# A hybrid encoder block with hierarchical experts: the routing taken tile by tile, with the engine's eight largest values and their places

## The reference

```python
gl = (xt @ w_group + b_group).astype(jnp.float32)
gp = jax.nn.softmax(gl, axis=-1)
g_onehot = jax.nn.one_hot(jnp.argmax(gl, axis=-1), N_GROUPS, dtype=jnp.float32)
g_w = jnp.sum(gp * g_onehot, axis=-1)
el = (xt @ w_expert + b_expert).astype(jnp.float32).reshape(-1, N_GROUPS, EXPERTS_PER_GROUP)
el_sel = jnp.einsum('nge,ng->ne', el, g_onehot)
ep = jax.nn.softmax(el_sel, axis=-1)
top_w, top_i = lax.top_k(ep, TOP_K)
top_w = top_w / jnp.sum(top_w, axis=-1, keepdims=True)
...
for gi in range(N_GROUPS):
    h = jax.nn.silu(jnp.einsum('nd,edf->nef', xt, w_gate[gi])) * jnp.einsum('nd,edf->nef', xt, w_up[gi])
    y = y + jnp.einsum('nef,efd->nd', h * combine[:, gi, :, None], w_down[gi])
```

## Time and profile before

| | us |
|---|---|
| median of 3 runs | 555.96 |
| lowest, highest | 554.34, 557.6 |
| the profiled execution | 554.07 |
| its span, first to last instruction | 552.0 |
| TensorE busy in it | 448.0 |
| VectorE busy | 108.8 |
| ScalarE busy | 80.7 |
| DMA, moved and mean | 217.68 MB, 394 GB/s |

### The profile page before, as it was taken

The page is one execution under the profiler, slowest core; times in us unless marked ns, Lnnn a source line. Parts: engine busy times, 40 slices in busy tenths (PEclk is TensorE's granted clock), DMA queues, the critical chain, the costliest instruction groups (busy, mean ns, idle before and its releaser), DMA issues.

```text
span 552.0 us, 6408 instructions
## 1 busy us (share of the span) xinstructions
PE 448.0 (81%) x2532; PEld 193.2 (35%) x2532; DVE 108.8 (20%) x348; ACT 80.7 (15%) x217; POOL 28.5 (5%) x61
## 2 busy tenths in 40 slices
PE   9999999999999978559999984952965485665794
PEld 3455554664353332133343521420213121311232
DVE  1028863261140310110210400300021000400012
ACT  1127663221110100000101001000000001000113
POOL 0242412100000000000000000000000000000000
PEclk9999999999999998789999988876877876986998
DMA  8989995969999999999999999999999999999993
GB/s 311 349 326 425 389 343 186 370 249 354 423 421 421 430 425 427 427 430 427 427 426 430 427 425 431 425 430 425 430 429 425 431 425 430 424 431 426 421 397 123
DMA packets 27374, 217.68 MB, mean 394 GB/s; under 512 B 5288, under 2 KB 8104, under 8 KB 13776
## 3 DMA queue, kind: packets, MB, share of 16 engines
q1 hardware_dynamic: 22976, 214.84, 93.8%
q10 hardware_dynamic: 4368, 2.42, 1.5%
HBM read 216.18 MB, written 1.06 MB: 394 GB/s over the span
## 4 chain that ended last, share of the span: by engine, by line
PE 48%; DMA 47%; another core or an unknown queue 2%; SPq 1%; issue 1%; DVE 1%; ACT 0%; DVEq 0%; POOL 0%
DMA ring<-in_w_up_dram 26%; DMA ring<-in_w_gate_dram 21%; PE bank L1478 17%; PE bank L1213 8%; PE bank L1301 5%; PE bank L1503 3%; PE bank L1439 2%; PE bank L1255 2%; PE bank L1279 1%; PE bank L1267 1%; PE bank L1533 1%; PE bank L1551 1%; SPq L340 1%; PE bank L1205 1%
## 5 line engine op out<-in xcount | busy, mean ns | idle before, releaser
L1478 PE MATMUL bank<-ring,head 128*32 128x512 f32 (+1 forms) x992 | 155.3, 677 | 68.8 <-DMA ring<-in_w_gate_dram 38.2
L1478 PEld LDWEIGHTS bank<-ring,head 128*32 128x32 f32 (+1 forms) x992 | 44.6, 128 | 170.0 <-issue 169.9
L1503 PE MATMUL bank<-ring,region_q 128*32 128x512 f32 (+1 forms) x480 | 75.5, 668 | 24.0 <-DMA ring<-in_w_down_dram 23.1
L1081 DVE COPY region_q<-bank 128x256 f32<-128x256 f32 x10 | 4.2, 424 | 300.5 <-PE bank L1457 300.5
L1503 PEld LDWEIGHTS bank<-ring,region_q 128*32 128x32 f32 (+1 forms) x480 | 22.1, 128 | 70.0 <-issue 69.4
L722 ACT ACTIVATE head<-bank 128x512 f32<-128x512 f32 x18 | 9.9, 595 | 238.3 <-PE bank L1533 231.7
L1213 PE MATMUL bank<-ring,head 128*128 128x512 f32 x96 | 43.6, 602 | 0.5 <-DMA ring<-in_w_in_dram 0.5
L1439 PEld LDWEIGHTS bank<-region_q,h 128*128 128x128 f32 x304 | 35.7, 192 | 9.1 <-issue 9.1
L1439 PE MATMUL bank<-region_q,h 128*128 128x128 f32 x304 | 38.5, 279 | 0.0
L1533 PE MATMUL bank<-head,region_q 128*128 128x512 f32 x72 | 33.3, 605 | 1.2 <-ACT head L722 1.2
L1301 PE MATMUL bank<-ring 128*128 128x512 f32 x64 | 29.7, 600 | 0.0
(11 more groups left out here) (198 smaller groups left out, 299.9 us busy)
## 6 DMA issues: line engine op xcount, KB each, us to landing
ring<-in_w_gate_dram SPq DMA_DIRECT2D x28, 2048.0 KB, 39.1
ring<-in_w_up_dram SPq DMA_DIRECT2D x28, 2048.0 KB, 38.9
ring<-in_w_down_dram SPq DMA_DIRECT2D x24, 2048.0 KB, 38.9
ring<-in_w_down_dram SPq DMA_DIRECT2D x12, 1024.0 KB, 13.8
ring<-in_w_up_dram SPq DMA_DIRECT2D x8, 1024.0 KB, 11.9
ring<-in_w_gate_dram SPq DMA_DIRECT2D x6, 1024.0 KB, 10.2
ring<-in_w_o_dram SPq DMA_DIRECT2D x2, 2048.0 KB, 11.9
ring<-in_w_in_dram SPq DMA_DIRECT2D x7, 512.0 KB, 8.0
```

What stands on the lines that cost most here:

```text
L1478: last = pe.matmul(ps[bank][rows, :], xgT[:, c, rows], slots[fill_slot(f + a)][:, c * F:(c + 1) * F], start=(c == 0), stop=(c == KC - 1))
L1503: last = pe.matmul(ps[bank + half][rows, :], hT[:, c, rows], down_cols(slots[fill_slot(f + a)], half, c), start=(c == 0), stop=(c == FC - 1))
```

## The change

VectorE takes tile 0 as soon as its logits are there and then tile 1. The groups' logits lie in a row of eight (`gl8`, padded with -1e30 by a `memset`), the eight largest come from `dve.max`, their places from `dve.max_index`. The places of the group make a mask over the 32 experts, the masked logits go through the same two operations, and the first two places give two one-hot rows (`hots`). `rank_tile(0)` and tile 0's two picks (`first_pick`) stand between tile 1's steps. The two exponentials are asked for together. On TensorE four of the five calls of `multiply_constants` go, tile 0's ranks, counts and the first six chunks of its gather stand ahead of tile 1's. The gathered chunks go to four banks by pairs (`FIRST_BANKS`), with a release for each pair. The order of the experts comes directly behind the picks, the weights and `weigh_picks` behind it. The fourth copy of turned rows goes to ScalarE.

```diff
+            act.wait_ge(h_turned, 4)
+            act.activation(hTr[:, 4:8, P:2 * P], ps[7][:].rearrange("p (c t) -> p c t", c=4), ACT.Copy).then_inc(hTr_act, 1)
+            act.wait_ge(exps_asked, 1)
+            act.activation(g_exp, g_off, ACT.Exp)
+            act.activation(e2, e2, ACT.Exp).then_inc(exps_ready, 1)
...
             def gathered_out(i):
-                act.wait_ge(gathered, 2 * i + (2 if i else 1))
+                if i:
+                    act.wait_ge(gathered, 2 * i + 3)
                 for c in range(4):
-                    last = act.activation(xgT[:, c, :], ps[GD0][:, c * P:(c + 1) * P], ACT.Copy, scale=g2_rows[:, c:c + 1])
+                    if i == 0 and c % 2 == 0:
+                        act.wait_ge(gathered, c // 2 + 1)
+                    last = act.activation(xgT[:, c, :], ps[GD0 if i else FIRST_BANKS[c // 2]][:, c * P:(c + 1) * P], ACT.Copy, scale=g2_rows[:, c:c + 1])
...
-            dve.wait_ge(h_turned, 4)
-            dve.tensor_copy(hTr[:, 4:8, P:2 * P], ps[7][:].rearrange("p (c t) -> p c t", c=4)).then_inc(hTr_dve, 1)
...
+            def best_group(t):
+                return mark(dve.max(g_max8[:, t, :], gl8[:, t, :]))
+
+            def group_place(t):
+                return mark(dve.max_index(g_at[:, t, :], g_max8[:, t, :], gl8[:, t, :]))
...
+            def group_only(t):
+                return mark(dve.scalar_tensor_tensor(here[:, t, :], off_group[:, t, :], NEG, el[:, t, :], ALU.mult, ALU.add))
...
+            k_g = group_logits(1)
+            expert_logits(1)
             after(k_g)
+            k_g = best_group(1)
+            k_rank = rank_tile(0)
             after(k_g)
+            k_g = group_place(1)
+            after(k_rank)
+            first_pick(0, 0)
             after(k_g)
+            k_off = other_groups(1)
+            first_pick(0, 1).then_inc(pick_first, 1)
+            after(k_off)
+            after(group_only(1))
+            after(best_experts(1))
+            after(expert_places(1))
+            two_hots(1).then_inc(hots_ready, 1)
+            dve.wait_ge(hots_ready, 1)
+            choose(1)
...
+            after(rank_tile(1))
+            first_pick(1, 0)
+            first_pick(1, 1).then_inc(pick_ready, 1)
...
             pe.wait_ge(chosen_ready, 1)
+            pe.matmul(ps[RANK0][:, 0:EXPERTS], upper, chosen[:, 0, :], start=True, stop=True).then_inc(ranked, 1)
+            pe.matmul(ps[RANK1][:, 0:EXPERTS], ones, chosen[:, 0, :], start=True, stop=False)
+            pe.matmul(ps[COUNTS][:, 0:EXPERTS], ones, chosen[:, 0, :], start=True, stop=False)
+            pe.matmul(ps[COUNT_COL][0:EXPERTS, 0:1], chosen[:, 0, :], ones[:, 0:1], start=True, stop=False)
+            multiply_constants(1, Y2)
+            pe.wait_ge(pick_first, 1)
+            first_gather(0, range(0, 4))
+            pe.wait_ge(hots_ready, 1)
...
             pe.wait_ge(pick_ready, 1)
+            first_gather(1, range(0, 2)).then_inc(gathered, 1)
+            first_gather(1, range(2, 4)).then_inc(gathered, 1)
+            pe.wait_ge(places_ready, 1)
+            pe.matmul(ps[ORDER][0:1, 128:128 + EXPERTS], expert_col, place_hot[0:EXPERTS], start=True, stop=True).then_inc(ordered, 1)
...
             first_gate(range(0, 4))
+            first_gather(1, range(4, 6)).then_inc(gathered, 1)
+            first_gather(0, range(6, KC))
+            first_gather(1, range(6, KC)).then_inc(gathered, 1)
             pe.wait_ge(xg_mid, 1)
```

More of the change, by code:

```diff
@@ new lines, in _ @@
+            k_w = mark(dve.tensor_scalar(w1, e2, 1.0, None, ALU.add))
+            after(k_key)
+            k_key = mark(dve.tensor_reduce(place[0:EXPERTS], key_above[0:EXPERTS], AX_X, ALU.add))
+            after(k_g)
+            k_g = mark(dve.reciprocal(gw, gsum))
+            after(k_key)
+            dve.tensor_tensor(place_hot[0:EXPERTS], iota1[0:EXPERTS, 0:EXPERTS],
+                              place[0:EXPERTS].broadcast_to([EXPERTS, EXPERTS]), ALU.is_equal).then_inc(places_ready, 1)
@@ L1106, in _ @@
+            dve.tensor_copy(counts, ps[COUNTS][:, 0:32])
+            dve.tensor_tensor(w_first, hots[:, :, 0, :], bcast(w1, 2, EXPERTS), ALU.mult)
+            link(dve.tensor_tensor(w_second, hots[:, :, 1, :], bcast(w2, 2, EXPERTS), ALU.mult))
+            link(dve.tensor_tensor(weight, w_first, w_second, ALU.add))
             gathered_out(0)
+            weigh_picks(rank1, weight, 0, 2)
             make_picks(rank1, 2, 2)
@@ L1433, in _, with first_gather @@
-            pe.matmul(ps[COUNTS][0:EXPERTS, 32:33], chosen[:, 1, :], ones[:, 0:1], start=False, stop=True).then_inc(counted, 1)
-            multiply_constants(1, GATE)
+            def first_gather(t, chunks):
+                for c in chunks:
+                    last = pe.matmul(ps[FIRST_BANKS[c // 2]][:, c % 4 * P:(c % 4 + 1) * P], h_cols[:, t, c, :], pick[:, t, :],
+                                     start=(t == 0 and c % 2 == 0), stop=(t == TT - 1 and c % 2 == 1))
+                return last
@@ L1436, in gather_chunks @@
+            first_gather(0, range(4, 6))
             def gather_chunks(b, chunks):
```

225 lines of the change are left out of this document (90 added, 135 removed).

## The result

| us | before | after |
|---|---|---|
| median (runs) | 555.94 (4) | 549.83 (4) |
| lowest, highest | 554.34, 557.6 | 549.45, 551.97 |
| profiled execution, its span | 554.07, 552.0 | 551.97, 549.7 |

The ratio of after to before is 0.9899, with a 95% interval of 0.9869 to 0.993: some 5.6 us faster. The medians themselves differ by 6.1 us, the profiled executions by 2.1 us only. That these two comparisons disagree by 4 us is what the experiments had to explain.

A forecast was written before the change was run, and what follows sets the result against it. The prediction took the expert-weight stream as the bound, standing still some 4.8 us during routing. Its steps put the order matmul at 115.2 against 118.61, 3.4 us earlier, giving 552.6 from the median 555.96; range 550.4 to 555.6.

The forecast's parts named there:

- pass-through: From stream restart to kernel end: a restart earlier by x ends the kernel earlier by x, up to 4.8 us.
- The prediction's own sign against the pass-through: In the changed profile: order matmul before 116 without the span shrinking as much would mean the pass-through is wrong.
- (a): Tile 0's new VectorE chain beside TensorE's work on tile 1: ten operations, 2.29 us, done at 110.11, no slack.
- (b): Tile 1's VectorE chain from its logits at 110.22 to the hot rows: sum 2.6 us, ready at 112.85.
- (c): From hot rows to picks: two rank matmuls, one rank read, two picks instead of four; picks ready at about 113.97.
- (e): Experts' order directly behind the picks: 1.23 us on VectorE, places ready at 115.2; order matmul 3.4 us earlier.
- (d): TensorE's gather: six calls of tile 0 (1.33 us) inside waits, four calls (0.89) behind the picks, to 114.86.
- (f): Work moved behind: two more gather calls between the first gate's halves, +0.45 us, not noticed by the DMA engines.
- Dear index operations: Rival in VectorE's routing: searches at 0.56 and maxima at 0.35 add 1.5 us; gain 1.9, time 554.1; chance 0.18.
- Closed gap: Rival at the stream's restart: the 4.8 us gap is gone entirely, time 551.2; chance 0.09.
- No effect on the end: Rival behind the restart: what follows eats the earlier restart, time within 1 us of 556; chance 0.06.
- Slower by the clock: Rival on TensorE: routing pauses halve its clock, three 3.4 us stretches cost 5.1, time 557.7; chance 0.07.

The follow-up runs named there:

- e15: Changed kernel without the one constant multiplication left in the routing; mixer's last loads to first piece 11.72 us against 12.04.
- e12: Changed kernel with the weight steps and weighted picks ahead of the experts' order again; mixer's last loads to first piece 14.00 us, 1.96 more.
- e10: Kernel before without its last constant multiplication; mixer's last loads to first piece 15.35 us, against 15.34 in the kernel before.
- e3: Changed kernel with two constant multiplication calls in TensorE's wait for the last unit's up slots; median 551.35 (10 runs).
- e6: Changed kernel with a third product of zeros at the start and two constant multiplications ahead of the last unit's up product; median 550.12 (6 runs).
- e8: e6 with four pieces instead of three for the first refilled gate slots; median 550.67, mixer's last loads to first piece 11.17 us.
- e9: e6 with 24 dependent dead copies ahead of tile 1's rank on VectorE; median 556.25 (12 runs), mixer's last loads to first piece 18.85 us.
- e11: Changed kernel with tile 0's rank and picks behind tile 1's choice, its gather behind tile 1's rank; last loads to first piece 12.38 us, 0.34 more.
- e7: e6 with both expert numbers read by SyncE ahead of the first piece; median 550.13, mixer's last loads to first piece 12.03 us.
- e17: e6 without the one constant multiplication left in the routing; median 550.2 (6 runs), mixer's last loads to first piece 11.72 us.
- e4: Changed kernel with twelve dependent dead copies ahead of tile 1's rank on VectorE; median 553.93 (12 runs), last loads to first piece 13.72 us.

## Why the prediction was right or wrong

**Bound, place and pass-through: right.** The stream is what ends the kernel; it started 3.30 us of R earlier and took the same 389.5 to 389.8 us. The prediction's own sign against the pass-through did appear, an order matmul before 116 (115.05) and a span that shrank by 2.3 only. It pointed the wrong way. The table takes the 2.3 apart: 0.3 from the start, 3.3 from R, 0.6 from the first piece to 50 MB, less 0.15 in the stream and 1.7 at the end.

**The size of the change's gain: right in sum, 3.4 against 3.30, by errors that cancel.** Counted from the pick-up of tile 1's logits (110.22 there, 109.83 here):

(a) Tile 0's chain: 2.29 forecast, 2.19 measured (107.57 to 109.76), level with TensorE as said. (The sum has nine terms for ten operations. The second read of logits, L978, has none in (a) or (b); it cost under 0.1.)

(b) To the hot rows: 2.63 forecast, 2.20 measured (109.83 to 112.03, where L1002 ends). The unknown operations were dear in the forecast. The eight largest take 0.16 to 0.20. The places are two instructions, as the Trainium skill, "VectorE: DVE Perf Modes", section "Two Vector instructions with no wait between them", lists them, and the trace agrees: 0.08 and 0.16 over eight values, 0.09 and 0.19 over 32, 0.23 and 0.27 from start to end, against my 0.32 to 0.35.

(c) From the hot rows to the last pick: 1.12 forecast, 1.81 measured (112.03 to 113.84). I let TensorE be free for tile 1's ranks at once. It was in tile 0's gather, and VectorE waited 0.67 us for the rank. This is the step that cost more (0.69) than (b) had won (0.43). The constants ahead of that gather are about half of the wait: without them, in e15, 0.35 us are left.

(e) The row of places: 1.23 forecast, 0.79 measured (113.84 to 114.63), since interleaved steps follow each other at 0.1. I made VectorE the one that sets the order's time; the chain says TensorE. In (d) I had given TensorE 0.89 from the last pick to the end of the gather; it took 1.21 (113.84 to 115.05), by luck almost exactly the 1.23 that I had put down for VectorE. That e12 makes VectorE late again shows how much (e) was worth. Of the constants that (d) has over the pick's arrival in the kernel before, e10 leaves nothing: taking them out alone gives 0.

(f) The 0.45 between the gate's halves is there: from the first piece to the first L376 load 10.26 us against 9.80. It did not reach the end, as said.

Together: 4.98 forecast from the pick-up to the order matmul, 5.22 measured, and 0.13 won back by an earlier pick-up and a quicker first piece.

**The time: wrong, and the step that failed is the last line of the sum,** "from it: 552.6", with the range below it, and not the gain of 3.4. I took the median of the runs to be the profiled execution plus a constant 1.9 us, and the scatter to be 1.6 to either side of any median. The 1.9 was no constant but two throws of the clock: at the start up to 2.7 us, near the end 1.7. Three of the first four runs of the changed kernel lie at 549.45 to 549.87. The traces of e3 and e6, with a quick start and a full clock at the end, are of runs of 550.25 and 549.81, and their lowest runs are 549.42 and 549.74. The three have no trace, so that they were such runs is inferred. Nor is it shown that this was mere chance: the three lowest of fourteen would fall into one given session of four in about 1% of cases (an estimate, 4 of 364 ways), so the quick start may be more frequent in one session than in another. That stays open. Ten more runs have a median of 552.86, 0.3 from the forecast; but that the first four could lie at 549.8 was part of what a range has to hold. The term that was too small is the scatter, 1.6 to either side: the changed kernel's fourteen runs lie between 549.45 and 553.52, 4.1 from end to end, and a median of four of them can fall near either end.

**Rivals.** Dear index operations: no, they were cheap. Closed gap: no, a gap of one us is left, and e8, which narrows it, brings nothing. No effect on the end: no. Slower by the clock: not here; it exists (e9, 2.6 us of R), with a pause ten times as long as any that the change makes in the routing. The stretch of 3.4 us by which the rival was priced stands in no row of this case.

## What to carry to other kernels

When a stream from memory sets the time, follow back what releases it and put on that path only what the release needs: keeping the weights out of the way of the experts' order was worth 2 us (e12), the interleaving of the tiles a third of one (e11). Give a wait that is filled with dummy work a second look after every speed-up, since the filler is then what is waited for. Before a difference of one per cent between two medians of a few runs is explained, take it apart into stages by the trace (start, routing, stream, end): the stage that the change touches repeated to 0.02 us, while the total scattered by five.

## What the runs showed of the hardware

I had not expected that the scatter of a kernel has so small a home: without fillers twelve identical products at the start take anything from 5.50 to 7.97 us (5.39 to 6.23 with the filler), and one product near the end takes 3.64 or 5.34 and nothing between, with the granted clock at 0.50 in it. A product of zeros of 192 columns at the start and two calls on constants near the end brought the scatter of the changed kernel from 3.3 us (10 runs) to 0.9 (e6), 2.4 (e7), 1.9 (e8) and 1.7 (e17), six runs each. Pauses of TensorE of 0.37 (e15), 1.53 (e4) and 1.91 us (e12) in the routing, and of 1.05 to 1.84 near the end, left its speed as it was; 2.19 to 2.45 near the end and 3.98 in the routing (e9) halved it. On VectorE the eight largest of eight or of 32 values took 0.16 and 0.20 us, their places 0.23 and 0.27.
